# Attention rounds that run on from pair to pair, with the wide matmuls between them on two PSUM banks of their own

## The reference, cut to what matters

```python
h = rmsnorm(x, norm_mix[i])
p = h @ w_in                                    # one input projection for all heads of the layer
tok = hgrn_branch(...)                          # layer 0: gated linear recurrence, 6 heads of 128
tok = swa_prompt(q, k, v, sinks)                # layer 1: 12 query heads of 64, 4 key/value heads,
                                                #   window 128 with a sink, head_rms on q and k
tok_s = swa_sample(q, k, v, buf_k, buf_v, ...)  # sample rows: 128 cached keys and the 4 new ones
mo = mem_attend(cq, mk, mv, q_norm)             # both layers: 4 heads of 64 over 256 memory keys
x = x + concat(tok, mo) @ w_out[i]
x = x + (silu(g) * u) @ w_ffn_out[i]            # g, u = rmsnorm(x) @ w_ffn_in[i]; 2816 wide
```

## Time and profile before

| | us |
|---|---|
| median of three runs | 3099.82 |
| the runs | 3109.3, 3099.82, 3081.87 |
| profiled execution, its own time | 3079.84 |
| its span, first to last instruction | 3078.0 |
| mean granted TensorE clock in it | 0.948 |

### The profile page before, as it was taken

The page is one execution under the profiler, slowest core; times in us unless marked ns, Lnnn a source line. Parts: engine busy times, 40 slices in busy tenths (PEclk is TensorE's granted clock), DMA queues, the critical chain, the costliest instruction groups (busy, mean ns, idle before and its releaser), DMA issues.

```text
span 3078.0 us, 41731 instructions
## 1 busy us (share of the span) xinstructions
PE 2868.6 (93%) x16482; PEld 2580.0 (84%) x16482; DVE 1295.8 (42%) x2031; ACT 653.5 (21%) x1068; POOL 641.9 (21%) x322
## 2 busy tenths in 40 slices
PE   5889999998899999999988898888789999999998
PEld 5779888897799999999977787767679999999997
DVE  4323444434544444444454334253454444444444
ACT  4311121211411111111123313241441111111110
POOL 5012332222421111221114001000142111112210
PEclk8889999998899999999998988888799999999999
DMA  4121011111121111111102121001012111111211
GB/s 156 28 62 43 23 41 49 50 36 29 42 55 41 41 41 41 41 51 51 55 21 62 35 62 28 15 14 45 12 38 56 46 41 41 41 41 46 56 28 57
DMA packets 186023, 135.34 MB, mean 44 GB/s; under 512 B 19616, under 2 KB 175456, under 8 KB 185888
## 3 DMA queue, kind: packets, MB, share of 16 engines
q1 hardware_dynamic: 181760, 129.69, 15.1%
q10 hardware_dynamic: 4160, 4.19, 0.4%
HBM read 124.61 MB, written 11.27 MB: 44 GB/s over the span
## 4 chain that ended last, share of the span: by engine, by line
PE 78%; PEld 9%; DVE 5%; issue 3%; ACT 2%; POOL 1%; PEldq 1%; DMA 1%; SPq 0%; DVEq 0%; ACTq 0%
PE ps L1245 41%; PE ps L1282 22%; PEld ps L1245 5%; PE ps L1434 3%; PEld ps L1553 2%; PE ps L1407 2%; PE ps L1419 2%; PE ps L1503 1%; PEld ps L1282 1%; POOL w_lo L488 1%; PEldq L1262 1%; PEld ps L1271 1%; DVE x L846 1%; PE ps L1459 1%; DVE normed_gained L843 1%
## 5 line engine op out<-in xcount | busy, mean ns | idle before, releaser
L843 DVE TENSOR_TENSOR x<-x,ps 128x512 f32<-128x512 f32 (+1 forms) x882 | 604.6, 686 | 913.1 <-PE ps L1282 891.7
L488 POOL TENSOR_TENSOR w_lo<-w_raw,w_hi 128x1024 fp32r<-128x1024 f32 x194 | 466.1, 2422 | 2172.7 <-ACT w_hi L484 2172.7
L1245 PE MATMUL ps<-hT_hi,w_hi 128*128 128x352 f32 x2976 | 719.9, 330 | 10.9 <-POOL w_lo L488 7.4
L1245 PE MATMUL ps<-hT_lo,w_hi 128*128 128x352 f32 x2976 | 711.0, 327 | 0.3
L1245 PE MATMUL ps<-hT_hi,w_lo 128*128 128x352 f32 x2976 | 708.4, 326 | 0.0
L1245 PEld LDWEIGHTS ps<-hT_hi,w_hi 128*128 128x128 f32 x2976 | 523.0, 192 | 39.9 <-POOL w_lo L488 7.7
L1245 PEld LDWEIGHTS ps<-hT_lo,w_hi 128*128 128x128 f32 x2976 | 524.9, 191 | 30.5 <-issue 2.7
L1245 PEld LDWEIGHTS ps<-hT_hi,w_lo 128*128 128x128 f32 x2976 | 524.3, 191 | 25.2
L1282 PE MATMUL ps<-w_hi,m_hi 128*128 128x512 f32 (+1 forms) x1060 | 429.6, 405 | 11.8 <-DVE m_lo L843 7.5
L1282 PE MATMUL ps<-w_lo,m_hi 128*128 128x512 f32 (+1 forms) x1060 | 425.6, 402 | 0.0
L1282 PE MATMUL ps<-w_hi,m_lo 128*128 128x512 f32 (+1 forms) x1060 | 423.6, 400 | 0.0
(11 more groups left out here) (225 smaller groups left out, 2379.9 us busy)
## 6 DMA issues: line engine op xcount, KB each, us to landing
w_raw<-in_w_ffn_in_dram SPq DMA_DIRECT2D x176, 256.0 KB, 3.2
w_raw<-in_w_ffn_out_dram SPq DMA_DIRECT2D x88, 256.0 KB, 3.7
w_raw<-in_w_in_hgrn_dram SPq DMA_DIRECT2D x52, 256.0 KB, 4.6
w_raw<-in_w_out_dram SPq DMA_DIRECT2D x32, 256.0 KB, 3.9
w_raw<-in_w_in_swa_dram SPq DMA_DIRECT2D x24, 256.0 KB, 3.8
x<-in_x_prompt_dram SPq DMA_DIRECT2D x8, 512.0 KB, 9.4
w_raw<-in_w_mem_kv_dram SPq DMA_DIRECT2D x16, 256.0 KB, 5.6
cache<-in_cache_mem_k_dram SPq DMA_DIRECT2D x4, 1024.0 KB, 7.3
```

Source lines behind the costliest of these rows:

```text
L488: nc.gpsimd.tensor_tensor(slot(1, s), raw[:, j3, :], slot(0, s).bitcast(F32), ALU.subtract).then_inc(w_lo, 1)
L843: return V_.tensor_tensor(out, a, b, op)
L1245: return mmul(ps[:, b0 + g, 0:TW], slot(a, s)[:, P * k:P * k + P], hT[b][:, k, TW * g:TW * g + TW], start=m < 3, stop=m >= 69)
```

## The change

Banks 0 and 1 hold the scores of one round, 2 and 3 its turn, 4 the rows and 5 the outs. Banks 6 and 7 are for everything else, taken in turn by a list of uses, `dense_uses`, written out ahead. Before a use TensorE waits until the use two before it on that bank has been read (`take`); readers wait for `full` and report `freed`. Scores have one set of banks now: a round's scores wait for the round before it.

- `project` does a projection in three groups of 384, 384 and 288 columns, one bank each; a group is squared by ACT and copied by DVE at once. The sums of squares are made per half (`half_sums`), and the square roots with them (`half_stds`).
- Pairs 1 to 4 are one loop of 36 steps (`pairs`). In a step TensorE does the parts of the rounds, and then wide work: keys and values in the steps of pair 1; in pair p the second half's projection, the sample chain of pair p-1, the outputs of pair p-1 (nine groups in each of two steps), and the first half's projection of pair p+1. Pair 4's last steps hold the outputs of pair 3 and its own sample chain.
- Keys are projected with tokens on the partitions; ACT squares them, DVE sums and scales, and TensorE transposes them back. `key_sums` and `key_norm` go.
- A sample cache's transposed keys are written over the cache itself, for the window once and not once per pair.
- Layer 0's pair 0 gets its sample chain and the first recurrence projections between its rounds; these are copied to SBUF.
- The memory outputs of layer 1 move into pair 2. The stores of the new window move on SP from the end of the weight loads to before job 12's load, and DVE waits for them in pair 2; the window caches are loaded from ACT's queue.

```diff
+def dense_uses():
+    ...
+    for p in range(2, NPAIR):
+        i = 2 * (p - 1)
+        u += [("qs", i), ("q", i + 1, 0), ("sc", p - 1), ("q", i + 1, 1), ("q", i + 1, 2), ("pt", p - 1),
+              ("qs", i + 1), ("pv", p - 1)]
+        if p < LAST_PAIR:
+            u += [("o", p - 1, G) for G in range(OUTG)] + [("q", i + 2, g) for g in range(TG)]
+    ...
 # SP
-                    if n == J_TOK:
-                        if L == 1:
-                            wait(sp, sT, 1, "pv")
-                            ...
+                    if L == 1 and n == J_PAIR:
+                        freed(sp, "vv", 4)
+                        freed(sp, "kw")
+                        store(new_swk_p[0, 0].rearrange("w h d -> w (h d)"), ktok[:, 0, :])
+                        ...
 # ACT
+            def half_stds(i):
+                half, b, n = i % 2, bank("qs", i), 2 * NPT
+                full(act, "qs", i)
+                nc.scalar.activation(HS[:, n * half:n * half + n], ps[:, b, 0:n], ACT.Sqrt, ...)
+                ...
+            def key_rows(t):
+                m, n = (P, 512) if t < 4 else (TS, 256)
+                full(act, "kk", t)
+                ...
+                A(ksq[0:m, 0:n], ps[0:m, bank("kk", t), 0:n], ACT.Square, kA, t, "sq")
+                wait(act, kS, t, "ss")
+                A(kst[0:m, 8:8 + n // HD], kst[0:m, 0:n // HD], ACT.Sqrt, kA, t, "std", ...)
 # DVE
+            def half_lo(p, half):
+                wait(dve, oA, 2 * p + half, "hi")
+                ...
+                if p == 1 and half == 1:
+                    dve.wait_ge(stored, 16 * NSTORE)
+                tt(mm[1][:, half, 0:SEQ], ..., ALU.subtract).then_inc(oV.sem, 1)
+            def pair_add(p, G):
+                i, n = G // 2, G % 2
+                full(dve, "o", p, G)
+                ...
+                tt(xs, xs, ps[0:rows(i), bank("o", p, G), :], ALU.add).then_inc(free_sem("o", p, G), 1)
 # PE
+            def take(*key):
+                u = USE[key]
+                if u >= 2:
+                    pe.wait_ge(dense_free[u % 2], u // 2)
+            def project(key, j, s, g):
+                c0, n = GROUPS[g]
+                if g == 0:
+                    pe.wait_ge(w_lo, j + 1)
+                take(*key)
+                for k in range(KT):
+                    for q, (a, b) in enumerate(PASS):
+                        ins = mmul(ps[:, bank(*key), 0:n], slot(a, s)[:, P * k:P * k + P], hT[b][:, k, c0:c0 + n], ...)
+                ...
+            def attend(S, r0, r1):
+                if S - 4 >= r0 and S % 2:
+                    prompt_out(S - 4)
+                if r0 <= S - 3 <= r1:
+                    prompt_rows(S - 3)
+                if r0 <= S - 2 <= r1:
+                    prompt_turn(S - 2)
-            def prompt_scores(r, half, pr, window):
-                if r % 8 >= 2:
-                    wait(pe, vM, r - 2, "max") if window else wait(pe, aE, r - 2, "exp")
+            def prompt_scores(r):
+                if r not in (0, 8):
+                    wait(pe, vM, r - 1, "max") if r > 16 else wait(pe, aE, r - 1, "exp")
+                ...
+            def pairs(J):
+                for S in range(8, 44):
+                    p = min(S // 8, LAST_PAIR)
+                    s, i, j = S - 8 * p, 2 * (p - 1), J + J_PAIR + 4 * (p - 2)
+                    attend(S, 8, 39)
+                    if p >= 2 and s == 0:
+                        half_sums(i)
+                    if S < 40:
+                        prompt_scores(S)
+                    ...
+                    if s < 3:
+                        project(("q", i + 1, s), j - 1, 1, s)
+                    if s == 0:
+                        sample_scores(p - 1)
+                    if s == 2:
+                        sample_turn(p - 1)
+                    if s == 3:
+                        half_sums(i + 1)
+                        sample_rows(p - 1)
+                    if p < LAST_PAIR:
+                        if s == 4 or s == 5:
+                            for G in range(9 * (s - 4), 9 * (s - 4) + 9):
+                                pair_out(p - 1, G, j)
+                        if s == 6:
+                            project(("q", i + 2, 0), j + 2, 0, 0)
+                            project(("q", i + 2, 1), j + 2, 0, 1)
+                        ...
```

More of the change, by code:

```diff
@@ L420, in _ @@
                         if h == 0:
-                            wait(sp, sT, 0, "pv")
+                            full(sp, "pv", 0)
                         else:
@@ new lines, in half_hi, with first_pair @@
+            def half_hi(p, half):
+                wait(act, vOT, 4 * p + 2 * half + 1, "ot")
+                if p >= 2:
+                    full(act, "o", p - 1, OUTG - 1)
+                A(mm[0][:, half, 0:SEQ], qb[(2 * p + half - 2) % 3 if p else half][:, 0:SEQ], ACT.Copy, oA, 2 * p + half, "hi")
+            def first_pair():
+                for S in range(12):
+                    if 2 <= S < 10:
+                        prompt_turn(S - 2)
+                    if S < 8:
+                        prompt_exp(S)
+                    if S < 2:
+                        for b in range(4 * S, 4 * S + 4):
+                            cache_turn(0, b)
+                    if S == 2:
+                        sample_exp(0)
+                sample_hi(0)
+                half_hi(0, 0)
+                half_hi(0, 1)
@@ L1196, in _ @@
                 dve.wait_ge(masks_in, 16)
[L1197 to L1201 removed]
+                head_gains(L, [qb[0][:, :], qb[1][:, :]], col(S_GQ + 1 + L))
+                query_norm(L)
+                wait(dve, qV, L, "n1")
                 if L == 0:
+                    first_pair()
                     adds(OUT0[L])
@@ new lines, in half_sums @@
+            def half_sums(i):
+                wait(pe, hSQ, i - 2, f"g{TG - 1}")
+                take("qs", i)
+                t, b = (qsq_a if i < 4 else qsq_b), bank("qs", i)
+                heads = cst[:, C_BLK:C_BLK + P].rearrange("p (h c) -> p h c", h=2)[:, :, 0]
+                for n in range(NPT):
+                    mmul(ps[:, b, 2 * n:2 * n + 2], t[:, P * n:P * n + P], heads, start=True, stop=True)
+                mmul(ps[:, b, 2 * NPT:2 * NPT + TS], cst[:, C_BLK:C_BLK + P], t[:, SEQ:T],
+                     start=True, stop=True).then_inc(full_sem("qs", i), 1)
@@ new lines, in pair_out @@
+            def pair_out(p, G, j):
+                i, n = G // 2, G % 2
+                if G == 0:
+                    pe.wait_ge(w_lo, j + 2)
+                    wait(pe, oV, 2 * p + 1, "lo")
+                    wait(pe, sLo, p, "lo")
+                take("o", p, G)
+                for q, (a, s, b) in enumerate([(a, s, b) for s in range(2) for a, b in PASS]):
+                    ins = mmul(ps[0:rows(i), bank("o", p, G), :], mm[b][:, s, P * i:P * i + rows(i)],
+                               slot(a, s)[:, 512 * n:512 * n + 512], start=q == 0, stop=q == 5)
+                ins.then_inc(full_sem("o", p, G), 1)
+                if G == OUTG - 1:
+                    pe.drain().then_inc(w_used, 2)
```

948 lines of the change are left out of this document (635 added, 313 removed).

## The result

The changed kernel takes 2979.11 us (median of 2976.28 to 2980.98), the old one 3097.47 beside it: a ratio of 0.9627, 95% interval 0.9601 to 0.9652. The forecast was 3018 in 2968 to 3066, faster; the time came out 39 us under it. The profiled executions are 2978.05 and 3079.84 us, 101.8 apart, where the sum had 81. (The medians lie 118 apart; the profiled execution of before is faster than each of its other runs.)

The account below looks back on a forecast made before the run. TensorE's work and waits bound the kernel: layer 1 at 401 work + 33 waits + 27 clock = 461 against 537.4, layer 0 5 less, so 81 off 3079.8, 2999; 3018 against the median, range 2968 to 3066.

Parts of the forecast that it names:

- the lockstep (B): Layer 1's rounds each keep their 2.25 us wait for exp and maximum: saving about 20, 3080 us; chance 0.14.
- D: Borders between layer 1's pairs: a wait at each first step holds the rounds, some 15 us each, 3065; chance 0.04.
- C: Layer 1: TensorE stays at 1.2 GHz for much of it, so slower, 3163 us at mean clock 0.70; chance 0.06.
- Work: Layer 1: TensorE's matmuls summed at full clock from rows of the old kernel, 401 us.
- Stalls: Layer 1: waits left on TensorE's path, 33 us, bounded by 8.5 and 72.
- the key chain: Pair 1: key groups' bank waits for square, sum, root and scaling, covered except twice: 4 us.
- the copies behind exp: Layer 1: memory cache transposes need ACT copies while ACT is in that step's exp: 3 us.
- the weight split before step 6: Layer 1: a wait for the weight split before step 6's projection, 1 us.
- in step 4 of each later pair DVE comes from splitting the half before: DVE then has four maxima before its first add while TensorE finishes two groups: 3 us, three times, 9.
- Clock: Layer 1: sample rows, half sums, start and short waits lower the granted clock, 27 us, between 0 and twice that.
- Rival A: The clock falls only where TensorE waits, so small streams cost nothing: 27 us less, 2991; chance 0.14.
- Layer 0: First scores to second weight's outputs: 98 us for 103.5, 5 less, between 0 and 15.

Follow-up runs that it names:

- the run without the streams: Changed kernel with sample rows of one sample of eight only and one sum of 16 columns for eight of two: 2952.7 us (0.9528).
- the kernel with the rows in the outputs: Changed kernel with the sample rows of pairs 2 to 4 moved from step 3 into the outputs: 2990.0 us (0.9659).
- the early split: Changed kernel with sample rows among the outputs and, ahead of them, output weight and (pairs 3, 4) the half before split sooner: 2984.9 us (0.9660).

## Why the prediction was right

**The mechanism held.** In pairs 1 to 4 rounds and wide work run on with no waits but the few listed above; the wait for exp that each step would show otherwise is 4.7 us. That refutes the lockstep (B), which needed a wait in each round; the borders between pairs show none either, against D. For C the clock would have had to be under 0.79; it is 0.91. That the total came within 20 us is in part luck: work and stalls were put too high by 29 together, the clock's loss too low by 9.

**The size: 441 for 461.** The three terms:

- Work, 401 foreseen, 385 found (TensorE's time by line, each piece weighted by the granted clock). Rounds were the most mis-sized term: 124.5 for 134.4. I took 1.97 for the rows of a round, from a row where they follow a gap; in the new kernel most follow other matmuls directly and take 1.73 or less. The allowance of 8 for small matmuls was 1. Sample scores were 17.5 for 21.2. Projections (72 for 71), keys and values (52 for 54.3), outputs (77 for 75.5) were right; half sums (12.4 for 10.1), sample rows (19.7 for 18.8) and transposes (8.6 for 7.7) were a little more.
- Stalls, 33 foreseen, 20 found. The start (4.1 for 4), the key chain (2.7 and 0.9 for 4), the copies behind exp (2.7 for 3), the window's transposes (1.6 for 1.5), the last softmax (2.2 for 2) and the tail (3.6 for 4.5) came nearly as put down; the weight split before step 6 (1) does not show, and of the drains' 4 about 2 do. The failed step is "in step 4 of each later pair DVE comes from splitting the half before ... 9": it was 0. I had not seen that the sample rows ahead of it, which run at the low clock, give DVE the time; when they are moved and the split is done earlier, 4.2 and 2.9 us of that very wait appear. (When they are moved alone, TensorE waits 9.8 us for the split before that.)
- Clock, 27 foreseen, 36 found. Sample rows and half sums do lower it, as counted, and longer than the 6 us that I took per stream: 14 to 17 us where one follows the other. The streams of pairs 2 to 4 and the short dips have 27 of the 36 (21 foreseen), 22 of it in those three places; the start and pair 1 have 9 (6 foreseen). Two experiments show the cause: with few narrow matmuls left the rounds hold 1.00, with the half sums thinned a third of the loss goes.

**Rival A** said that only waits lower the clock. The rows at 0.50 with 4.00 of 4.00 us busy speak against it, though waits do it too: in the run without the streams it falls in the 6.4 us wait. The Trainium skill says (TensorE: Matmul & The Clock Gate, What's actually happening) that the throttled state is the default and that being busy releases it. The wait agrees with that; the rows recorded as busy at 0.50 do not, and the measurement decides. (The profile models the ends of matmuls, so gaps too short to be recorded can't be excluded.) The time lies nearer to A's 2991 than to 3018, but by the terms above, not by A's reason: the clock's loss was there in full.

**Table loads.** ACT has 21 in the stretch (before: 7), the 14 more that were counted:

```profile
L696 ACT ACT_TABLE_LOAD x11 | 14.1, 1283 | 0.2
L652 ACT ACT_TABLE_LOAD x6 | 7.7, 1283 | 0.1
L574 ACT ACT_TABLE_LOAD x4 | 5.1, 1283 | 0.1
```

A load starts 0.02 us behind the instruction before it, and a function that is ready starts 1.30 us after the load's start:

```profile
1841.10 1.28 ACT L652 ACT_TABLE_LOAD   x1
1842.39 0.27 ACT L652 ACTIVATE q_row_rstd<-ps,params 128x16 f32<-128x16 f32 x1
```

So the 2.66 that the Trainium skill (ScalarE: Activation LUTs, What ACT_TABLE_LOAD costs) sets for a switch does not show here. The key chain's waits are 3.6 for the 4 foreseen.

**The queues.** SP's twenty stores took 0.26 to 0.82 us of issue each, from 1785.7 to 1793.7, and DVE has no wait for them.

**Layer 0: 5 foreseen, 2 found.** Between the marks of the earlier trace rows, first scores and second weight's outputs, it is 101.8 us (94.2 to 196.0) for 103.5, where 98 was foreseen. Both waits were in the sum and came about as large (8.2 for the cache transposes, foreseen as 8; 5.5 for the splits). Between these marks work at full clock falls by 5 us (77.8 to 72.8), idle time rises by 2.3 (12.4 to 14.7) and the clock's loss by 1 (13.2 to 14.2). The prediction gives no sum for its 98, so which of its terms was short stays open.

## What to carry to other kernels

If a chain of small steps has a fixed length, work out whether each step of another stream is longer than it: here 8 to 19 us stand against 5, and taking that away costs more than the whole gain. Two banks taken in turn were enough here, and the second is worth an add per group that follows another directly (0.94 us). Before a stream that looks harmful is moved, ask what it hides: with the rows moved and the split early, 7 us of clock loss went (36 to 29 by windows) and 9 us of waits came.

## What the runs showed of the hardware that was not expected

- The granted clock fell from 1.00 (2.4 GHz) to 0.50 (1.2 GHz) behind the half sums and within the sample rows though TensorE is recorded busy in all of 4.00 us. In 9 us of rounds with only a dozen narrow matmuls among them it held 1.00. 24 matmuls of 384 columns right behind the half sums did not prevent the fall: it came inside them (0.57 in 4 us).
- DVE's subtraction of 1024 columns took 2.53 us while POOL subtracted a weight (1839.7 to 1842.0), and 1.23 in the kernel where POOL had finished. The two rows, from the kernel with the rows in the outputs and from the early split:

```profile
1840.59 2.53 DVE L1020 TENSOR_TENSOR m_lo<-q_heads,m_hi 128x1024 fp32r<-128x1024 f32 x1 [1.20 <-ACT m_hi L575]
```

```profile
1844.48 1.23 DVE L1024 TENSOR_TENSOR m_lo<-q_heads,m_hi 128x1024 fp32r<-128x1024 f32 x1 [0.25 <-ACT m_hi L575]
```
